# A small transformer stack on one core: VectorE adds every second expert row of two chunks in place of every fourth

## What is computed

```python
def peer(h, w_query, query_gain, sub_keys_1, sub_keys_2, expert_down, expert_up):
    def block(hb):                                   # 128 tokens
        ...
        top_s, pos = lax.top_k(cand_s, 16)           # 8 heads x 16 experts
        experts = jnp.take_along_axis(cand_i, pos, axis=-1)
        gates = jax.nn.softmax(top_s, axis=-1)
        u = expert_down[experts]
        vv = expert_up[experts]
        act = jax.nn.gelu(jnp.einsum("thkd,td->thk", u, hb), approximate=False)
        return jnp.einsum("thk,thkd->td", gates * act, vv)
    out = lax.map(block, h.reshape(4, 128, 1024))
```

## Time and profile before

| what | us |
| --- | --- |
| median of 3 runs | 3593.21 |
| lowest and highest of them | 3591.1, 3606.76 |
| the profiled execution, whole | 3597.12 |
| its span, first to last instruction | 3594.6 |
| its mean granted TensorE clock | 0.941 of 2.4 GHz |

### The profile page before, as it was taken

The page is one execution under the profiler, slowest core; times in us unless marked ns, Lnnn a source line. Parts: engine busy times, 40 slices in busy tenths (PEclk is TensorE's granted clock), DMA queues, the critical chain, the costliest instruction groups (busy, mean ns, idle before and its releaser), DMA issues.

```text
span 3594.6 us, 34901 instructions
## 1 busy us (share of the span) xinstructions
PE 3066.4 (85%) x12138; PEld 2107.4 (59%) x12138; DVE 2162.4 (60%) x4488; ACT 1197.8 (33%) x2382; POOL 589.7 (16%) x540
## 2 busy tenths in 40 slices
PE   5989999798777889999898887997799777777777
PEld 4868888587555668887777762565456422222222
DVE  6655443776455454442353779876657979755555
ACT  3243222443444432222562254662222211211111
POOL 0000000000000000000000023333333354443442
PEclk9999999899888999999899998998999899999999
DMA  6534444243111324442321477897899799999997
GB/s 220 187 126 141 141 137 142 79 141 94 47 36 41 110 87 145 143 144 83 118 71 48 176 256 291 318 391 266 337 402 403 285 420 421 422 422 421 421 421 324
DMA packets 147549, 797.84 MB, mean 222 GB/s; under 512 B 16304, under 2 KB 18480, under 8 KB 81712
## 3 DMA queue, kind: packets, MB, share of 16 engines
q0 software_dynamic: 73728, 536.90, 37.4%
q1 hardware_dynamic: 69840, 251.69, 21.5%
q10 hardware_dynamic: 3808, 7.02, 0.5%
HBM read 793.46 MB, written 2.10 MB: 221 GB/s over the span
## 4 chain that ended last, share of the span: by engine, by line
PE 58%; DVE 18%; DMA 14%; ACT 5%; issue 4%; DVEq 0%; POOL 0%; SPq 0%; ACTq 0%
PE psum L153 57%; DMA tail<-in_experts,tail 14%; DVE tail L187 5%; ACT arena L164 3%; DVE tail L170 2%; ACT L164 2%; DVE arena L182 2%; DVE tail L193 1%; DVE tail L182 1%; DVE tail L190 1%; DVE tail L196 1%; DVE region L170 1%; DVE tail L205 1%; PE psum L158 1%; ACT region L164 1%
## 5 line engine op out<-in xcount | busy, mean ns | idle before, releaser
L153 PE MATMUL psum<-tail,arena 128*128 128x512 f32 (+2 forms) x3652 | 1316.6, 509 | 305.2 <-ACT arena L164 273.7
L153 PE MATMUL psum<-rounded,rounded 128*128 128x512 f32 x5496 | 1293.8, 396 | 39.8 <-DVE rounded L182 27.2
L153 PEld LDWEIGHTS psum<-tail,arena 128*128 128x128 f32 x3652 | 687.0, 199 | 885.0 <-issue 829.5
L153 PEld LDWEIGHTS psum<-rounded,rounded 128*128 128x128 f32 x5496 | 1036.8, 190 | 279.9 <-issue 56.4
L216 POOL DMA_INDIRECT tail<-in_experts,tail x512 | 569.6, 1112 | 1837.3 <-PE psum L153 924.7
L187 DVE CUSTOM_DVE_ANT_0 tail<-tail 128x1024 f32<-128x1024 f32 x512 | 626.2, 1224 | 294.3 <-DMA tail<-in_experts,tail 292.0
L170 DVE TENSOR_TENSOR rounded<-arena,rounded 128x1024 fp32r<-128x1024 f32 (+2 forms) x285 | 316.5, 1111 | 346.7 <-ACT rounded L164 346.5
L164 ACT ACTIVATE tail<-tail 128x1 f32<-128x1 f32 (+1 forms) x544 | 115.5, 213 | 1035.1 <-DVE tail L187 860.6
L164 ACT ACTIVATE rounded<-arena 128x1024 fp32r<-128x1024 f32 (+2 forms) x317 | 291.9, 939 | 446.0 <-DVE arena L170 238.8
L153 PE MATMUL psum<-arena 128*128 128x1 f32 (+3 forms) x792 | 195.7, 371 | 77.3 <-ACT arena L164 47.1
L164 ACT ACT_TABLE_LOAD x189 | 242.5, 1283 | 12.1 <-PE psum L153 6.7
(11 more groups left out here) (82 smaller groups left out, 1561.3 us busy)
## 6 DMA issues: line engine op xcount, KB each, us to landing
arena<-in_ada SPq DMA_DIRECT2D x136, 512.0 KB, 3.9
arena<-in_fin SPq DMA_DIRECT2D x88, 512.0 KB, 4.2
arena<-in_win SPq DMA_DIRECT2D x56, 512.0 KB, 3.3
arena<-in_fout SPq DMA_DIRECT2D x32, 512.0 KB, 3.6
arena<-in_mxbc SPq DMA_DIRECT2D x32, 512.0 KB, 4.1
arena<-in_pq SPq DMA_DIRECT2D x32, 512.0 KB, 7.3
arena<-in_ain SPq DMA_DIRECT2D x24, 512.0 KB, 4.8
arena<-in_mz SPq DMA_DIRECT2D x16, 512.0 KB, 3.8
```

The costliest lines, as they stand in the source:

```text
L153: return self.e.matmul(o, a, b, start=start, stop=stop, skip_group_check=skip)
```

## The change

One line of `own_add` is another. In chunks 0 and 1 (n < 256) VectorE takes every odd s from 25 to 123, 50 experts in each chunk, where it took every fourth from 25 to 125, 26 experts. The bound of 124 keeps the chunk's last experts with TensorE. For chunks 2 and 3 the seven experts of each (s = 25, 41, ... 121) stay the same.

```diff
         def own_add(n):
 
             s = n % 128
-            return s >= 24 and (s % 4 == 1 if n < 256 else s % 16 == 9)
+            return 24 <= s < 124 and (s % 2 == 1 if n < 256 else s % 16 == 9)
```

## The result

The changed kernel takes 3603.76 us (median; 3600.22 to 3611.23) and the kernel before, measured beside it, 3596.7 us (3588.73 to 3606.76). The ratio is 1.0022, with a 95% interval of 1.0014 to 1.0029: 7 us or 0.2% slower, which is under the 0.5% named ahead and inside the range of 3579 to 3612. The forecast of no real change held. Its point was 3594.3 us, 1.1 us slower than before; the measured time is 9.5 above it, 3.5 of which are the kernel before itself (3596.7 in place of 3593.2). Its terms held only in part: two stretches in which it expected a gain (experts 56 to 64 and 64 to 88) were lost, and the term for the inversion was too small.

A forecast was written before the change was run, and what follows sets the result against it. In chunks 0 and 1 the bound changes by stretch between VectorE, TensorE, their turns and transfers; behind expert 256 transfers bind. 19.5 us lost against 4.7 + 13.7 won: 1.1 us slower, 3594.3 us, range 3579 to 3612.

The forecast's parts named there:

- The bound behind expert 256: From expert 256 on the transfers bind: 658 us as before, and earlier gains or losses come out one to one.
- Step 1: Experts 24 to 48, 48 to 56 and 196 to 228: VectorE binds and pays each add in full, 19.5 us lost.
- Step 2: Experts 56 to 96: TensorE is full, its relief ends at the DMA's share; 4.7 us won.
- Rival B: Experts 56 to 96: the DMA share is no wall, VectorE is next; 12.4 us won, 3586.6 us; chance 0.15.
- Step 3: Inversion, experts 96 to 128: without the odd expert's add TensorE's long step starts earlier; 13.7 us won.
- Step 4: Experts 152 to 196 and 228 to 256: the transfers cover both sides, nothing won or lost.
- rival C: Gathers on GpSimd are held by VectorE's new adds: up to 35.5 us lost, up to 3630 us; chance 0.04.
- Rival A: Inversion, experts 96 to 128: TensorE's lower clock takes back the gain, 18.9 us slower, 3613 us; chance 0.13.

The follow-up runs named there:

- the inversion alone: The kernel before with every second expert from 88 to 123 of chunk 0 added on VectorE, all else as before: 3578.48 us, ratio 0.9956.

## Why the prediction was right, and where it wasn't

**The bound behind expert 256** was right: 658 us became 659, and the differences of chunks 0 and 1 come out at the end.

**Step 1, VectorE binds.** Right: 18.8 us lost in the three stretches where 19.5 were forecast. Experts 24 to 48 and 196 to 228 grew by 6.6 and 11.2 us with their waits unchanged at 0.4 and 1.6, and taking adds away there gives the time back. Two sizes were off. The add of an expert follows the dot of the next, so that of expert 47 lies behind the border at 48: five in the stretch, 1.33 each, and the one of 47 in the next. In 196 to 228 the eight cost 1.40 each and not 1.30; VectorE's distance was read off one pair in chunk 0 and used for both.

**Step 2, "where TensorE is full but the transfers nearly are, the gain ends at the DMA's share".** This failed. Experts 56 to 96 were to win 4.7 us and lost 5.4. I took TensorE's 96% and the DMA's 0.99 for the bound and left VectorE out, since it was busy for 80% only. But VectorE's idle time there was made almost wholly of waits for ScalarE. Beside the 11.4 us for the copies in 11 steps, these are the rest of its waits in experts 56 to 88 before, and below them what stands beside the 11.7 us after:

```profile
DVE tail L170 <- ACT tail L164: 6.5, 3, 4.2
DVE tail L187 <- DMA tail<-in_experts,tail: 0.9, 2, 0.7
```

```profile
DVE tail L170 <- ACT tail L164: 6.9, 2, 4.3
```

18.8 us became 18.6, though TensorE had eight adds less to do. Busy time and waits together fill 108 of 110.5 us before, and the 9.7 us that the stretch grew by are the 9.9 by which VectorE's busy time grew. So VectorE had no slack for eight more adds. The two experiments show that TensorE and VectorE both bind there: eight adds more on either of them makes experts 56 to 88 over 8 us longer. What the DMA's share allows was never reached: it fell from 0.99 to 0.87 in 64 to 88. Rival B had the same root and falls with it: it priced VectorE by its busy time.

**Step 3, the inversion.** The mechanism was right, seen row by row: the step starts 1.8 us behind the even expert's add, and VectorE's own add lies in the wait that it shortens. The size was too small: 20.9 us in place of 13.7, and past the upper bound of 18 that was set for it. In 104 to 120 I took 2.1 us for each group of four, and 2.5 went (56.6 to 46.7): VectorE's waits went nearly to nothing, and 16.8 us of waits less 4 x 1.3 for the adds is 11.6 at most. In 96 to 104 I took the same 2.1 twice, and 9.1 went. The forecast took the waits of 104 to 120 for all; those of 96 to 104 in the kernel before are longer:

```profile
DVE tail L170 <- PE psum L153: 6.1, 1, 6.1
DVE tail L182 <- PE psum L153: 5.4, 2, 4.9
```

All 11.5 us are gone in the changed kernel, and the two new adds took 2.3 of them. The clock there rose from 0.75 to 0.90 at the same time. Its part can't be told apart: the kernel without adds in 24 to 48 has 4.1 us less at 0.89 with the same instructions, but the inversion alone has 8.5 us less at only 0.82, with 0.4 us of waits left.

**Step 4, the full transfers.** Right for 152 to 196 (0.3 us). Behind 228 the changed kernel took 2.0 us more, but kernels that keep the old split there took up to 1.7 more as well, so no cost of the new adds is shown there.

**The gathers, rival C.** The hold is there, and where VectorE binds it costs nothing. GpSimd's line in experts 196 to 228, before and after (busy us and mean ns of one, then its idle time):

```profile
L216 POOL DMA_INDIRECT tail<-in_experts,tail x34 | 38.3, 1126 | 86.9 <-PE psum L153 81.7 <-DVE tail L182 3.1 <-issue 2.1
```

```profile
L216 POOL DMA_INDIRECT tail<-in_experts,tail x32 | 43.9, 1371 | 88.2 <-PE psum L153 54.8 <-DVE tail L182 28.4 <-issue 5.0
```

An issue lasts 1371 ns in place of 1126. Over the whole trace of the changed kernel an issue that starts while VectorE is in a dot lasts 1.40 us in the mean (194 of them), in an own add 1.52 (38), and beside neither 0.95 (280). The dot and the own add each read two tiles in SBUF. This agrees with the rule of the Trainium skill (page "SBUF — State Buffer", section "Who interferes with whom") that a VectorE instruction with two SBUF inputs contends with a GpSimd instruction that reads SBUF. GpSimd is idle for two thirds of the stretch all the same, and VectorE never waits for a gather there.

**Rival A, the clock,** did not come: the inversion's clock is 0.90 and 0.96 after. Over all, the first two chunks ran at 0.87 in place of 0.92, but what fell is in stretches where VectorE binds (0.70 in 24 to 48, 0.82 in 196 to 228), in 152 to 196 (0.88), whose length didn't move, and in 64 to 88 (1.00 to 0.88), where ScalarE and so VectorE no longer wait for TensorE. No cost of it is seen.

Counted from expert 0, the sum came out 6.7 us too low. Experts 56 to 96 were 10.1 us worse than forecast and the inversion 7.2 better; these two misses stand against each other, and the remaining 4 are small ones, most of them behind expert 128, where the stretches differ by as much between kernels with the same split there. Each of the two large misses lay outside the bounds set for its term (0 to 6.4 and 5 to 18 us). That the total was right is in part luck.

## What to carry to other kernels

A split of work between two engines wants to be set stretch by stretch: one share for two chunks won 21 us where one engine waited for the other and lost it where the receiving engine had no waits at all. Before work is given to an engine, its list of waits counts and not its busy share. In experts 56 to 88 a wait that came again in each step from a hop over a third engine was no slack; in the inversion a wait for the very engine that was relieved was. And an engine that is full for a short stretch may still take work if nobody waits for its results there and it has room behind.

## What the runs showed of the hardware

A TensorE that is busy for 98% at its full clock may still have room: in experts 196 to 212 it was busy 60.8 of 61.8 us, took four more adds of 1.9 us and the stretch became 5.2 us shorter. It fell 6.5 us further behind and made up for it in the next stretch. In experts 56 to 88, at 96%, it had no room, since VectorE's steps wait for its products. The share doesn't tell the two apart; the lists of waits do.

The granted clock in a short stretch can differ with the same instructions: the same eight experts took 34.6 us at 0.75 and, in one kernel with other adds ahead of them, 30.4 at 0.89.

An issue of a gather on GpSimd lasted 0.95 us when it started beside no dot and no own add of VectorE, and 1.40 to 1.52 us when it started beside one.
